# The chunked scan of an RWKV-7 mixer reordered: wider TensorE products, narrow norms, gate product after the first chain step

## The reference

```
sa = S kk_t
S  = S * w_t - sa (kk_t * a_t)' + v_t k_t'
y_t = S r_t                      # summed over both directions, latent tokens only
...
kk = (k * k_k) / max(sqrt(sum((k * k_k)^2)), 1e-12)       # per head and token
k_dir = k * (1 + (a - 1) * k_a)
w  = exp(-exp(-softplus(-lw) - 0.5))                      # lw, a: low-rank products ("lora")
yn = (y - mean) / sqrt(var + eps) * ln_w + ln_b           # per head and token
out = ((yn + bonus) * g) @ w_o,  bonus = sum(r * k_dir * r_k) * v
```

## Time and profile before

| | us |
|---|---|
| median of 3 runs | 2684.48 |
| lowest, highest | 2682.06, 2690.17 |
| the profiled execution, its time | 2696.97 |
| its span, first to last instruction | 2695.2 |
| TensorE busy in the span | 2350.2 (87%) |
| VectorE busy | 1019.5 (38%) |
| ScalarE busy | 640.1 (24%) |
| GpSimd busy | 836.0 (31%) |
| mean granted TensorE clock | 0.932 |

### The profile page before, as it was taken

How to read it: one execution, slowest core, us unless ns; L and a number is a source line. 1 busy time by engine, 2 the same in 40 slices (tenths; PEclk the granted TensorE clock), 3 DMA queues, 4 the chain that set the end, 5 groups by cost and what they waited for, 6 DMA issues and landing times. The chain is left out here.

```text
span 2695.2 us, 53413 instructions
## 1 busy us (share of the span) xinstructions
PE 2350.2 (87%) x23840; PEld 1946.5 (72%) x23840; DVE 1019.5 (38%) x1482; ACT 640.1 (24%) x952; POOL 836.0 (31%) x699
## 2 busy tenths in 40 slices
PE   5899977989699999999489957888888858999997
PEld 3778754555499999999269936776777746788786
DVE  4100076890400000122692045777777641200123
ACT  4110165421400000122321123333333212211111
POOL 2233200100144444343054412222222205466562
PEclk8999988989799999999599968999999978999998
DMA  5555510001021111111123411111211111222231
GB/s 219 209 203 203 209 49 17 0 31 48 16 71 62 62 62 62 56 62 48 26 79 110 138 51 39 37 40 39 40 40 38 22 64 63 77 94 93 86 98 67
DMA packets 139278, 204.26 MB, mean 76 GB/s; under 512 B 87783, under 2 KB 97511, under 8 KB 131912
## 3 DMA queue, kind: packets, MB, share of 16 engines
q1 hardware_dynamic: 139080, 201.26, 23.1%
HBM read 183.93 MB, written 17.30 MB: 75 GB/s over the span
## 5 line engine op out<-in xcount | busy, mean ns | idle before, releaser
L258 POOL CAST TMP_r<-WR 128x1024 fp32r<-128x1024 f32 x120 | 126.9, 1058 | 757.3 <-DMA WR<-in_ffn_w_dram 437.9
L277 PE MATMUL PS<-H_r,TMP_r 128*128 128x384 f32 (+1 forms) x1088 | 331.1, 360 | 15.1 <-DVE Y_r L492 15.1
L277 PE MATMUL PS<-Y_r,TMP_r 128*128 128x384 f32 (+1 forms) x1088 | 330.3, 358 | 3.7 <-DVE H_r L492 3.7
L260 POOL TENSOR_TENSOR WR_r<-WR,TMP_r 128x1024 fp32r<-128x1024 f32 x120 | 290.0, 2416 | 9.6
L415 DVE TENSOR_TENSOR P<-TMP,PS 128x768 f32 (+1 forms) x44 | 36.1, 821 | 563.0 <-PE PS L277 563.0
L277 PEld LDWEIGHTS PS<-H_r,TMP_r 128*128 128x128 f32 x1088 | 202.1, 190 | 33.6 <-DVE Y_r L492 17.3
L277 PEld LDWEIGHTS PS<-Y_r,TMP_r 128*128 128x128 f32 x1088 | 201.8, 190 | 19.3 <-DVE H_r L492 4.0
L277 PE MATMUL PS<-H_r,WR_r 128*128 128x384 f32 x736 | 191.6, 342 | 0.0
L268 POOL CAST TMP_r<-WR 128x1024 fp32r<-128x1024 f32 x68 | 86.4, 1271 | 322.8 <-DMA WR<-in_rw_w_rkv_dram 165.3
L270 POOL TENSOR_TENSOR WR_r<-WR,TMP_r 128x1024 fp32r<-128x1024 f32 x68 | 165.3, 2431 | 5.4
L398 ACT ACTIVATE TMP<-PS 128x768 f32<-128x768 f32 (+1 forms) x44 | 31.1, 706 | 526.5 <-PE PS L277 526.5
(11 more groups left out here) (289 smaller groups left out, 4433.1 us busy)
## 6 DMA issues: line engine op xcount, KB each, us to landing
WR<-in_ffn_w_dram SPq DMA_DIRECT2D x88, 512.0 KB, 3.5
TMP<-in_mod_w_dram SPq DMA_DIRECT2D x40, 1024.0 KB, 4.9
WR<-in_down_dram SPq DMA_DIRECT2D x44, 512.0 KB, 3.6
WR<-in_mix_w_in_dram SPq DMA_DIRECT2D x24, 512.0 KB, 7.0
WR<-in_rw_w_rkv_dram SPq DMA_DIRECT2D x24, 512.0 KB, 4.2
P<-in_mod_w_dram SPq DMA_DIRECT2D x4, 2048.0 KB, 21.9
vkr_dram<-extra SPq DMA_DIRECT2D x16, 384.0 KB, 4.8
scan_front<-vkr_dram SPq DMA_DIRECT2D x16, 384.0 KB, 3.3
```

The costliest lines, as they stand in the source:

```text
L258: nc.gpsimd.tensor_copy(hi, raw).then_inc(weights_hi, 1)
L260: nc.gpsimd.tensor_tensor(lo, raw, hi.bitcast(F32), ALU.subtract).then_inc(weights_split, 1)
L277: last = nc.tensor.matmul(PS[:, bank + b, 0:h1 - h0], w, x[:, h0:h1], start=k + p == 0, stop=k == CT - 1 and p == 2)
```

## The change

- `lora` takes one k at a time and alternates the two directions, which lie on partitions 0 to 63 and 64 to 127.
- ok_e and obv_e become `solve`: entering keys and the value product lie side by side for the moving operand (`beside`), 128 columns a product, in three marks oo_0, oo_1 (chunks 0 to 7 of a direction) and oo_2 (the rest). ScalarE evicts each with one instruction of 1024 columns.
- m_e and r become mr_0, mr_1 (transition and query step side by side) and mr_2 (the four context chunks).
- K, C and D become KD_e (added keys by queries and entering keys, 128 columns) and CK_e (C, and K of the context chunks). VectorE masks them in four instructions (mK, mD, mC, mL) for two (mK, mCD).
- The two norms are turned: `turned_sums` gives one sum per token and head (12 or 8 columns); ScalarE takes the root, VectorE maximum and reciprocal, ScalarE spreads them (kwide, vwide) and TensorE transposes them back (kr, vr).
- ys adds into the banks in which yt lies; ScalarE copies the sum out, and VectorE's addition goes.
- From VectorE to ScalarE: the first keys of a chunk (first), the chunk ends (ends), rate, acc_0.
- New order: both l0 ahead of w16 and both l1 behind it; A_1 after oo_1; rt, kd and kt after the transitions; KD_0 ahead of step 2; bonus and gate (cg) behind step 1, as before; kk, kr, BV_1 and vr at the end of the round.

```diff
-            (1, "l00 l01"), (0, "w16_0 w16_1"), (1, "l10 l11"), (0, "x16_0 y16_0 x16_1 y16_1 w32_0 w32_1 y32_0 y32_1"),
-            (1, "A_0"), (0, "ok_0 obv_0 ok_1 obv_1 m_0 m_1"), (1, "A_1"), (0, "n_0 n_1 r yt"),
-            (0, "c0_1 c1_1 cg c0_2 c1_2"), (1, "K_0"), (0, "c0_3 c1_3"), (1, "CD_0"), (0, "c0_4 c1_4"), (1, "K_1"),
-            (0, "c0_5 c1_5"), (1, "CD_1"), (0, "c0_6 c1_6"), (1, "tV"), (0, "c0_7 c1_7"), (1, "tB_0"),
-            (0, "c0_8 c1_8"), (1, "tK_0"), (0, "c0_9 c1_9"), (1, "tB_1"), (0, "c0_10 c1_10"), (1, "tK_1"),
-            (0, "ys"), (1, "kT_0"), (2, "kk"), (1, "kT_1"), (0, "mean"), (1, "BV_0 BV_1"), (0, "var")))
+            (1, "l00 l10"), (0, "w16_0 w16_1"), (1, "l01 l11"), (0, "x16_0 y16_0 x16_1 y16_1 w32_0 w32_1 y32_0"),
+            (1, "A_0"), (0, "y32_1 oo_0 oo_1"), (1, "A_1"), (0, "oo_2 mr_0 mr_1 mr_2 n_0 yt n_1"),
+            (0, "c0_1 c1_1 cg"), (1, "KD_0"), (0, "c0_2 c1_2"), (1, "CK_0"), (0, "c0_3 c1_3"), (1, "KD_1"),
+            (0, "c0_4 c1_4"), (1, "CK_1"), (0, "c0_5 c1_5"), (1, "tV"), (0, "c0_6 c1_6"), (1, "tB_0"),
+            (0, "c0_7 c1_7"), (1, "tK_0"), (0, "c0_8 c1_8"), (1, "tB_1"), (0, "c0_9 c1_9"), (1, "tK_1"),
+            (0, "c0_10 c1_10"), (1, "kT_0"), (0, "ys"), (1, "kT_1"), (0, "mean"), (2, "kk"), (1, "BV_0"), (0, "var"),
+            (2, "kr"), (1, "BV_1"), (0, "vr")))
...
+            (1, "scan_0"), (0, "w16_0 w16_1"), (1, "scan_1"), (0, "x16_0 y16_0 x16_1 y16_1"), (1, "kin_0 ba_0"),
+            (0, "w32_0 w32_1"), (1, "bt_0"), (0, "y32_0 y32_1"), (1, "kin_1 ba_1 bt_1 mA_0 mA_1"),
+            (0, "m_0 r_0 m_1 r_1"), (1, "rt_0 kd_0"), (0, "m5_0 m5_1"), (1, "kt_0 rt_1"), (0, "n_0"),
+            (1, "kd_1 kt_1"), (0, "n_1 st0_1 st1_1"), (1, "acc_1"), (0, "bonus st0_2 st1_2"), (1, "mK_0 mD_0"),
+            (0, "st0_3 st1_3"), (1, "mC_0 mL_0"), (0, "st0_4 st1_4"), (1, "accr"), (0, "st0_5 st1_5"), (1, "mK_1 mD_1"),
+            (0, "st0_6 st1_6"), (1, "mC_1 mL_1"), (0, "st0_7 st1_7 st0_8 st1_8 st0_9 st1_9 st0_10 st1_10 cen"),
+            (2, "kmax krec"), (0, "rec"), (2, "kmul"), (0, "f1 f2 z")))
...
+            (1, "t00 t10 t01 t11 ep_0 en_0 ends_0 rate_0 first_0 ep_1 en_1 ends_1 rate_1 first_1"),
+            (0, "oo_0 oo_1 oo_2"), (1, "acc_0"), (0, "gt"), (1, "tV tB_0 tK_0"), (2, "kc ksq"), (1, "tB_1 tK_1 kT_0"),
+            (0, "ys"), (1, "kT_1"), (0, "sq"), (2, "kroot"), (1, "bv_0"), (0, "groot"), (2, "kwide"), (0, "vwide"), (1, "bv_1")))
...
+            def beside(first, second):
+                assert first.tensor is second.tensor and second.offset > first.offset
+                return strided(first, (second.offset - first.offset, 2), (1, TC))
...
+            def solve(i, name, turns):
+                b = back(name, i)
+                for k, (e, j) in enumerate(turns):
+                    for h in range(2):
+                        for q, qr in enumerate(H2):
+                            last = nc.tensor.matmul(PS[qr, b + h, 128 * k:128 * k + 128], XY[qr, 2 + e, h, j, :],
+                                                    beside(KINT[qr, e, h, j, :], BVT[qr, e, h, j, :]),
+                                                    start=True, stop=True)
+                PEM.done(last, name, i)
...
+            def turned_sums(bank, src, groups):
+                for j in range(groups):
+                    last = nc.tensor.matmul(PS[:, bank, 2 * j:2 * j + 2], src[:, 128 * j:128 * j + 128],
+                                            HONES[:, 0:128:64], start=True, stop=True)
+                return last
```

More of the change, by code:

```diff
@@ L1952, in hybrid_dit_kernel @@
         PEM = Marks(pe_done, (
[6 rows of a table removed]
-        DV = Marks(dve_done, (
[6 rows of a table removed]
-            (0, "st0_10 st1_10 ysum cen"), (2, "kmax krec kmul"), (0, "rec f1 f2 z")))
-        AC = Marks(act_done, (
-            (1, "t00 t01 ep_0 en_0 t10 t11 ep_1 en_1"), (0, "ok_0 obv_0 ok_1 obv_1 yt gt"),
-            (1, "tV tB_0 tK_0 tB_1 tK_1"), (2, "kc ksq"), (1, "kT_0"), (2, "kroot"), (1, "kT_1"), (0, "sq"),
-            (1, "bv_0 bv_1"), (0, "groot")))
-        PO = Marks(pool_done, ((1, "s00 s01 s10 s11 zero sub turn"),))
-        FRONT = ("l00 l01 l10 l11 A_0 A_1 cg K_0 CD_0 K_1 CD_1 tV tB_0 tK_0 tB_1 tK_1 kT_0 kk kT_1 BV_0 BV_1").split()
[7 rows of a table added]
+        DV = Marks(dve_done, (
[6 rows of a table added]
+            (2, "kmax krec"), (0, "rec"), (2, "kmul"), (0, "f1 f2 z")))
+        AC = Marks(act_done, (
[3 rows of a table added]
+        PO = Marks(pool_done, ((1, "s00 s10 s01 s11 zero sub turn"),))
+        FRONT = ("l00 l10 l01 l11 A_0 A_1 cg KD_0 CK_0 KD_1 CK_1 tV tB_0 tK_0 tB_1 tK_1 kT_0 kT_1 kk BV_0 kr BV_1").split()
         FRONT_TURN = {at: k for k, at in enumerate([at for at in PEM if at[0] in FRONT])}
@@ L1977, in hybrid_dit_kernel @@
         FRONT_FREE = {"l00": (AC, "t00"), "l01": (AC, "t01"), "l10": (AC, "t10"), "l11": (AC, "t11"),
-                      "A_0": (DV, "mA_0"), "A_1": (DV, "mA_1"), "cg": (AC, "gt"), "K_0": (DV, "mK_0"),
-                      "CD_0": (DV, "mCD_0"), "K_1": (DV, "mK_1"), "CD_1": (DV, "mCD_1"), "kk": (AC, "kroot"),
-                      "BV_0": (AC, "bv_0"), "BV_1": (AC, "bv_1")}
-        BACK = "w16_0 w16_1 x16_0 y16_0 x16_1 y16_1 w32_0 w32_1 y32_0 y32_1 ok_0 obv_0 ok_1 obv_1 m_0 m_1 n_0 n_1 r yt".split()
+                      "A_0": (DV, "mA_0"), "A_1": (DV, "mA_1"), "cg": (AC, "gt"), "KD_0": (DV, "mD_0"),
+                      "CK_0": (DV, "mL_0"), "KD_1": (DV, "mD_1"), "CK_1": (DV, "mL_1"), "kk": (AC, "kroot"),
+                      "kr": (DV, "kmul"), "BV_0": (AC, "bv_0"), "BV_1": (AC, "bv_1")}
+        BACK = "w16_0 w16_1 x16_0 y16_0 x16_1 y16_1 w32_0 w32_1 y32_0 y32_1 oo_0 oo_1 oo_2 mr_0 mr_1 mr_2 n_0 yt n_1".split()
+        BACK_FREE = {"oo_0": (AC, "oo_0"), "oo_1": (AC, "oo_1"), "oo_2": (AC, "oo_2"), "mr_0": (DV, "r_0"),
+                     "mr_1": (DV, "r_1"), "mr_2": (DV, "m5_1")}
         def front_bank(name, n):
@@ new lines, in transition_rest @@
+            def transition_rest(i):
+                b = back("mr_2", i)
+                pe.wait_ge(act_done, AC["oo_2", i])
+                for e in range(2):
+                    for j in range(4, 6):
+                        at = 128 * e + 64 * (j - 4)
+                        for p, pr in enumerate(H2):
+                            for h, hr in enumerate(H2):
+                                last = nc.tensor.matmul(PS[hr, b + p, at:at + 64], OO[pr, e, h, j, 0, :],
+                                                        TOKB[pr, e, j, hr], start=True, stop=True)
+                PEM.done(last, "mr_2", i)
@@ new lines, in outputs_carried @@
+            def outputs_carried(i):
+                pe.wait_ge(dve_done, DV["st1_10", i])
+                for ch in range(NLAT):
+                    for e in range(2):
+                        was = order(e)[order(e).index(ch) - 1]
+                        at = 64 * (ch // 2)
+                        for hr in H2:
+                            last = nc.tensor.matmul(PS[hr, 2 + ch % 2, at:at + 64], NE[hr, e, was % 2, was // 2, :],
+                                                    RSTEP[hr, ch % 2, e, ch // 2, :], start=False,
+                                                    stop=ch >= NLAT - 2 and e == 1)
+                PEM.done(last, "ys", i)
@@ L2225, in scan_pe @@
[L2225 to L2232 removed]
+                        level("x16", e, "w16", Ym, Wm)
@@ L2291, in scan_pe @@
-                    PEM.done(last, "yt", i)
-                    pe.wait_ge(dve_done, DV["r", i])
+                    solve(i, "oo_2", [(e, j) for e in range(2) for j in (4, 5)])
+                    transition(i, 0)
+                    transition(i, 1)
+                    transition_rest(i)
+                    states(i, 0)
+                    pe.wait_ge(dve_done, DV["mL_1", i])
+                    outputs_inside(i)
+                    states(i, 1)
+                    pe.wait_ge(dve_done, DV["n_1", i])
@@ L2532, in scan_dve @@
             for i, n, c in ROUNDS:
+                if here(n):
+                    sums(n, 0)
                 if here(i):
```

552 lines of the change are left out of this document (313 added, 239 removed), and 6 rows, old and new, of the table DV.

## The result

| | before | after |
|---|---|---|
| median, us | 2685.38 (10 runs) | 2697.72 (10 runs) |
| lowest, highest | 2681.17, 2690.99 | 2692.45, 2701.02 |
| ratio after / before | | 1.0034, 95% interval 1.0022 to 1.0046 |
| profiled execution, its span | 2696.97, 2695.2 | 2698.04, 2696.2 |
| busy us: TensorE, VectorE, ScalarE, GpSimd | 2350.2, 1019.5, 640.1, 836.0 | 2341.2, 945.5, 663.6, 848.5 |

The change made the kernel 0.34% slower, 9 us (the text goes by the ratio, whose interval is 6 to 12 us; the medians of the table stand 12 us apart). 2670.5 was predicted, in a range of 2646 to 2692, and the measured time lies outside it. The two profiled executions differ by 1.1 us only: that of before stood 11.6 us over its median of ten, and took 7.3 us more ahead of the scan and 1.5 us more behind it.

A forecast was written before the change was run, and what follows sets the result against it. The prediction took TensorE as nearly the bound, with a 69 us loop over VectorE, SP and GpSimd close behind. Entry 4, rounds 3.5 and last round 6.5 made 14 us off the 2684.48 median: 2670.5 us, range 2646 to 2692.

The forecast's parts named there:

- The entry: Ahead of the first recurrence: A_1's mask done earlier without the 4.95 us reciprocal, 4 us gained (2 to 6).
- The last round and the exit: From the last recurrence on: shorter wait at the first x16, fewer issue gaps, shorter end, 6.5 us gained (4 to 8).
- the term for the lower clock: Added to each middle round for stretches at the lower clock: 0.7 us, plus 2.5 us once for round 0.
- slower: the clock: Rival: idle in chain and tail drops TensorE's clock, two more 3.4 us stretches a round; round 74.3, 2694 us; chance 0.16.
- Both signs of being wrong: Middle rounds of the scan not within 70 to 71.7 us, or their granted clock outside 0.96 to 1.0.
- Head: Middle round from first lora product to chain step 1: 37.8 us, against 46.7 in the kernel before.
- Chain: Middle round from chain step 1 to step 10: 18.2 us against 15.0, as VectorE's masks hold TensorE.
- Tail: Middle round from chain step 10 to the next lora product: 13.7 us against 11.1, TensorE idle 2.7 before kr.
- Issue gaps: TensorE's gaps among many 64-column products: most of 28.2 us gone, 0.5 us a round left, none over 1 us at the states.
- The lora pairs: Lora products of the two directions overlap in alternating row halves: 1.5 us for each group of four, against 2.8.
- The wide grams and solves: TensorE's 128-column products in the head and chain: KD 0.9 us, CK 0.85, a solve of 16 products 1.85.
- The loop over SP: Masking A_1, block transfers, GpSimd's inversion and transfers back: 62 us against 71 for the next recurrence, 9 us of slack.

The follow-up runs named there:

- e1_fill: The changed kernel with dummy products of no effect in three idle places of TensorE a round, ahead of tV, tB_0 and kr; 0.32% faster than the changed kernel.
- e10_idle: The kernel before with TensorE made to wait ahead of tV and tB_0 for two added ScalarE copies each round; 0.78% slower than the kernel before.
- e3_table: The changed kernel with a one-column root on ScalarE ahead of the copy of ys, loading the root's table early; ratio 1.0038 to the kernel before.
- e14: The kernel before with the narrow norms and the paired lora alone; ratio 0.9963 to the kernel before.
- e7: The changed kernel with VectorE's direction-1 masks a chain step earlier, accr behind step 6, and ScalarE's kc and ksq behind tK_1's copy; ratio 0.9922 to the kernel before.

## Why the prediction was wrong

By the prediction's own sum the scan should have been 14 us shorter, and it is 9.8 longer, 23.8 off. The entry gained 5.3 us for 4 forecast (1632.88 - 1559.70 against 1645.46 - 1566.96); in part that is luck, since this one execution had 39 us at the lower level there and that of before 56. The last round and the exit, from the last recurrence to z, gained 63.2 - 59.2 = 4.0 for 6.5. The rounds are the rest: 518.6 for 496.0, 22.6 off.

**The step that failed is the term for the lower clock.** The prediction gave it 0.7 us a round, taking over the one stretch of 3.4 us that a round had before, and 2.5 us once for round 0: 7.4 us in all. A round had 9.1 us of it (63.4 in seven), which by 0.44 us each is 27.9. So 20.5 of the 22.6 are this term: 16.5 for the 37.4 us that came new, and 4.0 because the sum put too low a price on the 26.0 us that were there before. The mechanism was named, as the rival "slower: the clock": idle in chain and tail lets the clock fall; it decides from two more stretches of 3.4 us a round. It was one and a half, 5.3 us. The price of a stretch, 1.7, came out as 1.5. What was wrong is the chance of 0.16 that it got. The argument against it was that rounds before were granted 0.98, and that says nothing of a round with 12 us of idle (72.3 - 60.4) at other places than the 11 of before. That the lower clock took the time rests on three things: the rounds of one execution lie within 0.7 us of one line with it, the executions of each kernel show it in their mean clock, and e1_fill took it away by adding work. Both signs of being wrong that the prediction gave came: the middle rounds lie outside 70 to 71.7 us, and their clock went down to 0.89. What drew the lower clock stays open. That idle in general draws it is not shown: e10_idle added 2.4 us of idle a round to the kernel before and drew almost none.

**The rest, some 2 us, is the round at full clock,** where larger errors of the sum cancel. The round of the timeline above is 72.3 for 70.9, or 70.8 for 70.2 without the lower clock:

- Head 38.75 for 37.8. 0.6 of it is there at the first x16, 6.8 for 6.2: the first scan took 2.37 us, not 1.75.
- Chain 18.0 for 18.2. The waits fell where they were forecast: KD_1 0.81, tV 1.74, tB_0 1.39.
- Tail 15.55 for 13.7. kr's transposes took 1.32 for 0.85, BV_1 2.68 for 1.61: 1.5 is the lower clock, which the forecast had added separately.
- Issue gaps 1.7 us a round, 0.5 forecast, the longest 2.4 where none over 1 was to be left.

Here are VectorE's first scan, ScalarE's two table loads of a round with the root between them, and GpSimd's second pair of products in that round:

```profile
1932.48 2.37 DVE L2583 TENSOR_TENSOR_SCAN scan_front<-extra,scan_front 128x768 f32<-128x768 f32 x1 [1.49 <-POOL scan_front L2085]
...
1992.93 1.28 ACT L2531 ACT_TABLE_LOAD   x1
1994.23 0.18 ACT L2531 ACTIVATE scan_small<-PS 128x12 f32<-128x12 f32 x1
...
2001.27 1.28 ACT L2442 ACT_TABLE_LOAD   x1
```

```profile
1936.07 3.06 POOL L2085 TENSOR_SCALAR scan_front<-scan_front 128x768 f32<-128x768 f32 x2 [2.83 <-ACT scan_front L2442]
```

GpSimd's pair takes 3.06 us where the first of the round takes 1.63, beside VectorE's second scan; the scans take 2.37 and 2.03, and 1.75 in each of the 14 between the recurrences of rounds 0 and 7 before:

```profile
1797.13 1.75 DVE L2472 TENSOR_TENSOR_SCAN scan_front<-extra,scan_front 128x768 f32<-128x768 f32 x1
```

The Trainium skill's page "SBUF — State Buffer", section "Who interferes with whom", has a VectorE instruction with two inputs in SBUF contend with a GpSimd instruction that reads SBUF. The scans have two such inputs, and the lengthened pairs agree with it.

**What was right.** The lora pairs (1.56 for 1.5). The wide grams and solves cost what was forecast, start to start: 0.93 for KD (0.9; its row is 1.10 long), and two solves are 3.68 long (1.85 each). kr starts 10.65 us behind step 10 (10.6 forecast) and the idle before it is for ScalarE, but 1.18 us and not 2.7, as TensorE's own products ahead of it ran longer. The table loads take 1.28 us and the root starts 0.02 us behind: the drain of 1.38 us that the Trainium skill's page "ScalarE: Activation LUTs", section "What ACT_TABLE_LOAD costs", adds to each is not in this trace, and e3_table found no gain in hiding a load. VectorE has 45.7 us a round (45 forecast). The loop over SP had its slack: no round but the first waited for the inverse. At full clock the stretch came out near the forecast, 491 for the 489 that 496.0 leaves without its 7.4, and near that of the kernel before, 488; the table's last column can't tell them apart.

**Where the gain went.** The parts that were to pay do pay, where VectorE is out of the way: narrow norms with paired lora give 0.37% (e14). The rest of the change, wide products and the new order, brought fewer issue gaps and in their place 20 us of waits for masks in six rounds. Those are the price of an order on VectorE and ScalarE and not of the change's idea: with two moves in that order (e7) the whole is 0.78% under the kernel before. Against the changed kernel its stretch is 20 us shorter at full clock and has 26 us less at the lower level. The wide products and the new order of TensorE were not run apart, so what each is worth stays open.

## What to carry to other kernels

When a change takes work from TensorE and leaves it waiting in its place, read the granted clock by stage and price a change in it: in a round of 72 us each us at 1.2 GHz cost 0.44, and the reordering brought 5.3 us more of them a round. Two parts that each free one engine can be worth nothing or less alone (the lora: +0.39%, the norms 0) and 0.37% together; test them in pairs before one is given up. And where a wait is removed, look for the queue that it was hiding: the masks' order gained 0.33% alone and 1.12% once the keys' squares, which stood behind a load that SP held back, moved as well.
